# Columns of neighbouring weight tiles woven together in a two-layer decoder kernel

## What is computed

```python
qkv = (h @ w_qkv).reshape(B, S, 3, N_HEADS, HEAD_DIM)      # layer 0: 2048 x 6144
return out @ w_o                                           # both layers: 2048 x 2048
proj = h @ w_in                                            # layer 1: q, k, v, qi, ki, wi
u = h @ w_up                                               # both layers: 2048 x 11264
return (jax.nn.silu(gate) * val) @ w_down                  # both layers: 5632 x 2048
```

## Time and profile before

| | |
|---|---|
| median of 2 runs | 2218.64 us (2217.64 to 2219.65) |
| span of the profiled execution | 2216.0 us |
| outside the span, to the median | 2.6 us |
| TensorE busy with matmuls | 2209.4 us, 12470 matmuls |
| VectorE, ScalarE busy | 1484.4 us, 1177.3 us |
| weights loaded | 406.70 MB on SyncE's queue, 56.5% of the 16 DMA engines' time |
| granted TensorE clock | full in all of the span |

### The profile page before, as it was taken

The page is one execution under the profiler, slowest core; times in us unless marked ns, Lnnn a source line. Parts: engine busy times, 40 slices in busy tenths (PEclk is TensorE's granted clock), DMA queues, the critical chain, the costliest instruction groups (busy, mean ns, idle before and its releaser), DMA issues.

```text
span 2216.0 us, 34772 instructions
## 1 busy us (share of the span) xinstructions
PE 2209.4 (100%) x12470; PEld 1935.2 (87%) x12470; DVE 1484.4 (67%) x1753; ACT 1177.3 (53%) x1409; POOL 14.3 (1%) x21
## 2 busy tenths in 40 slices
PE   9999999999999999999999999999999999999999
PEld 8888898888888888888899888888888888888887
DVE  7666556677777777555578888667777777774443
ACT  7565555555555555444455466555555555553333
POOL 0000000000000000000010000000000000000000
PEclk9999999999999999999999999999999999999999
DMA  7555555555555555565566544555555656566664
GB/s 270 166 168 177 171 162 181 195 185 190 189 193 186 189 190 191 190 190 189 191 212 198 177 157 139 161 183 191 182 198 181 194 184 198 180 193 201 201 199 136
DMA packets 113829, 411.55 MB, mean 186 GB/s; under 512 B 12769, under 2 KB 13537, under 8 KB 113761
## 3 DMA queue, kind: packets, MB, share of 16 engines
q1 hardware_dynamic: 112320, 406.70, 56.5%
q10 hardware_dynamic: 1008, 2.30, 0.3%
q0 software_dynamic: 432, 1.57, 0.2%
HBM read 408.42 MB, written 2.10 MB: 185 GB/s over the span
## 4 chain that ended last, share of the span: by engine, by line
PE 99%; DMA 0%; SPq 0%; DVE 0%; ACT 0%; issue 0%; DVEq 0%
PE psum L1301 99%; DMA raw<-w_all 0%; PE psum L1621 0%; PE psum L1557 0%; DVE w_lo L747 0%; ACT w_hi L289 0%; SPq L237 0%; SPq L235 0%; DVE upad L822 0%; SPq L236 0%; SPq L234 0%; DVEq L83 0%
## 5 line engine op out<-in xcount | busy, mean ns | idle before, releaser
L747 DVE TENSOR_TENSOR w_lo<-raw,w_hi 128x1024 fp32r<-128x1024 f32 x769 | 935.6, 1224 | 678.6 <-ACT w_hi L289 672.8
L1301 PE MATMUL psum<-xg,w_hi 128*128 128x512 f32 (+1 forms) x3936 | 1358.3, 392 | 1.9 <-DVE w_lo L747 1.0
L289 ACT CAST w_hi<-raw 128x1024 fp32r<-128x1024 f32 x770 | 803.1, 1049 | 771.4 <-PE psum L1301 767.6
L1301 PE MATMUL psum<-xg,w_lo 128*128 128x256 f32 (+1 forms) x3920 | 1090.8, 278 | 0.0
L1301 PEld LDWEIGHTS psum<-xg,w_hi 128*128 128x128 f32 x3936 | 736.0, 187 | 156.7 <-issue 2.2
L1301 PEld LDWEIGHTS psum<-xg,w_lo 128*128 128x128 f32 x3920 | 742.6, 189 | 2.6 <-issue 2.2
L1301 PE MATMUL psum<-hid,w_hi 128*128 128x512 f32 x704 | 244.1, 391 | 0.0
L1301 PE MATMUL psum<-w_hi,hid 128*128 128x512 f32 x704 | 217.9, 390 | 0.0
L1301 PE MATMUL psum<-hid,w_lo 128*128 128x256 f32 x704 | 197.4, 280 | 0.0
L1301 PE MATMUL psum<-att,w_hi 128*128 128x512 f32 x512 | 178.8, 393 | 0.0
L1301 PEld LDWEIGHTS psum<-hid,w_hi 128*128 128x128 f32 x704 | 131.7, 187 | 28.6
(11 more groups left out here) (176 smaller groups left out, 1062.9 us busy)
## 6 DMA issues: line engine op xcount, KB each, us to landing
raw<-w_all SPq DMA_DIRECT2D x770, 512.0 KB, 3.8
xres<-x_in SPq DMA_DIRECT2D x3, 512.0 KB, 9.0
cst<-consts_in ACTq DMA_DIRECT2D x2, 768.0 KB, 6.6
raw<-w_all SPq DMA_DIRECT2D x2, 256.0 KB, 3.6
xres<-x_in SPq DMA_DIRECT2D x2, 256.0 KB, 3.8
out_t<-part POOLq DMA_DIRECT2D x1, 512.0 KB, 7.3
out_t<-conv POOLq DMA_DIRECT2D x1, 512.0 KB, 7.4
out_t<-gates POOLq DMA_DIRECT2D x1, 512.0 KB, 7.0
```

Of the source, the lines that this page charges most:

```text
L289: act.copy(w_hi[:, c % RING, :], raw[:, c % RING, :]).then_inc(hi_ready, 1)
L747: dve.tensor_tensor(w_lo[:, c % RING, :], raw[:, c % RING, :], f32(w_hi[:, c % RING, :]), ALU.subtract).then_inc(lo_ready, 1)
L1301: return pe.matmul(o, lhsT, rhs, start=start, stop=True, skip_group_check=True)
```

## The change

The host permutes the output features of the weights that `proj` and `proj_index` use as stationary operands (`_woven`): in each group of two tiles (four in the second output projection) column `j` of tile `a` goes to place `step * j + a`. On the chip the tile is then read with that step (`column_tile`), and what is multiplied with what is the same as before. Pieces, their order and their sizes stay, and so do the loads, the splits and all the instructions of ScalarE, VectorE, SyncE and GpSimd. TensorE's instructions stand in the same order with the same shapes, but for the line numbers; the step inside the access pattern of the stationary operand is all that differs.

Not woven are the KI projection (its pieces have a single tile for each row, step 1), the weighting of the indexer, and the weights that are moving operands (the values of both layers, the down projection of layer 1).

```diff
+            def column_tile(buf, s, row, ct, step):
+
+                if step == 1:
+                    return buf[:, s, row + ct * P:row + (ct + 1) * P]
+                if step == 4:
+                    return buf[:, s, row + ct:row + 4 * P:4]
+                pair = row + ct // 2 * 2 * P
+                return buf[:, s, pair + ct % 2:pair + 2 * P:2]
...
-                        w = slice(kk * cols + ct * P, kk * cols + (ct + 1) * P)
+                        hi, lo = (column_tile(buf, s, kk * cols, ct, step) for buf in (w_hi, w_lo))
...
-                        mm(psum[:, bank0 + ct, :], w_hi[:, s, w], act_in[:, k, :], first and kk == 0)
-                        last = mm(psum[:, bank0 + ct, 0:T], w_lo[:, s, w], act_in[:, k, 0:T])
+                        mm(psum[:, bank0 + ct, :], hi, act_in[:, k, :], first and kk == 0)
+                        last = mm(psum[:, bank0 + ct, 0:T], lo, act_in[:, k, 0:T])
...
-                        w = slice(kk * 256 + ct * P, kk * 256 + (ct + 1) * P)
+                        hi, lo = (column_tile(buf, s, kk * 256, ct, 2) for buf in (w_hi, w_lo))
...
-            out_groups(BASE_WO[1], 1, 8, att, 0, wo1_ready, l1_tail)
+            out_groups(BASE_WO[1], 1, 8, att, 0, wo1_ready, l1_tail, step=4)
...
+def _woven(w, step):
+
+    k, n = w.shape
+    w = w.reshape(k, n // (step * P), step, P)
+    return np.ascontiguousarray(w.transpose(0, 1, 3, 2)).reshape(k, n)
...
-               _pieces(v, 2, 512), _pieces(k, 4, 256), _pieces(q, 4, 256),
-               _pieces(a["wo1"][0], 2, 512)) + mlp(1))
+               _pieces(v, 2, 512), _pieces(_woven(k, 2), 4, 256), _pieces(_woven(q, 2), 4, 256),
+               _pieces(_woven(a["wo1"][0], 4), 2, 512)) + mlp(1))
```

More of the change, by code:

```diff
@@ L1301, in mm, with proj @@
                 return pe.matmul(o, lhsT, rhs, start=start, stop=True, skip_group_check=True)
-            def proj(c, i, per, bank0, act_in, kts, k0_, cols, first, by_tile=False, upper_free=None):
+            def column_tile(buf, s, row, ct, step):
[5 more added lines that the diff above has]
+                return buf[:, s, pair + ct % 2:pair + 2 * P:2]
+            def proj(c, i, per, bank0, act_in, kts, k0_, cols, first, by_tile=False, upper_free=None, step=2):
                 if by_tile:
@@ L1336, in proj_index @@
                             pe.wait_ge(xg_ready, 11)
-                        w = slice(kk * 256 + ct * P, kk * 256 + (ct + 1) * P)
+                        hi, lo = (column_tile(buf, s, kk * 256, ct, 2) for buf in (w_hi, w_lo))
                         both = xg[:, k0_ + kk, :].rearrange("p (a t) -> p a t", a=2)[:, :, TI:T]
-                        mm(out2, w_hi[:, s, w], both, first and kk == 0)
-                        last = mm(psum[:, bank0 + ct, 0:n], w_lo[:, s, w], xg[:, k0_ + kk, TI:T])
+                        mm(out2, hi, both, first and kk == 0)
+                        last = mm(psum[:, bank0 + ct, 0:n], lo, xg[:, k0_ + kk, TI:T])
                 last.then_inc(piece_used, 1)
@@ L1380, in settle, with out_groups @@
                     mm(psum[:, bank, 0:P], xg[:, 0, 0:P], xg[:, 1, 0:P], True)
-            def out_groups(base, layer, per, src, n0, ready, tail=None):
+            def out_groups(base, layer, per, src, n0, ready, tail=None, step=2):
                 for g in range(4):
@@ L1389, in out_groups @@
                         upper = ready(e) if g == 0 else None
-                        proj(base + g * per + e, None, 0, 4 * (g % 2), src, 2, 2 * e, 512, e == 0, upper_free=upper)
+                        proj(base + g * per + e, None, 0, 4 * (g % 2), src, 2, 2 * e, 512, e == 0, upper_free=upper, step=step)
                         if tail and g == 0:
@@ L1543, in mlp_layer @@
                     out_groups(base + UP, layer, FT // 2, hid, 4 + 2 * UPG,
-                               lambda e: hid_ready(layer, e))
+                               lambda e: hid_ready(layer, e), step=2)
                 else:
@@ L1666, in _ @@
             for e in range(2):
-                proj(L1_KI + e, None, 0, 2, xg, 8, 8 * e, P, e == 0)
+                proj(L1_KI + e, None, 0, 2, xg, 8, 8 * e, P, e == 0, step=1)
                 if e == 0:
@@ L1746 @@
     flat = lambda *p: [q.reshape(-1, P, PIECE) for q in p]
-    qkv = [_pieces(a["qkv"][0][:, n * D:(n + 1) * D], 4, 256) for n in range(3)]
+    qkv = [a["qkv"][0][:, n * D:(n + 1) * D] for n in range(3)]
+    qkv = [_pieces(qkv[n] if n == 2 else _woven(qkv[n], 2), 4, 256) for n in range(3)]
     two = _pieces(a["qkv"][0][:, 2 * D + 256:3 * D - 256], 2, 512)
@@ L1758, in mlp @@
         up = a["up"][layer]
-        both = np.concatenate([_pieces(up[:, :FF], 2, 512), _pieces(up[:, FF:], 2, 512)], axis=1)
-        return flat(both, _pieces(a["dn"][layer], 2, 512))
-    qip = _pieces(qi, 4, 256)
+        both = np.concatenate([_pieces(_woven(up[:, :FF], 2), 2, 512), _pieces(_woven(up[:, FF:], 2), 2, 512)], axis=1)
+        return flat(both, _pieces(a["dn"][layer] if layer else _woven(a["dn"][layer], 2), 2, 512))
+    qip = _pieces(_woven(qi, 2), 4, 256)
     w_all = np.concatenate(
-        flat(*l0, _pieces(a["wo0"][0], 2, 512)) + mlp(0)
+        flat(*l0, _pieces(_woven(a["wo0"][0], 2), 2, 512)) + mlp(0)
         + flat(qip[:1], _pieces(kk, 8, P), _pieces(np.pad(np.concatenate([wi, wi], axis=1), ((0, 0), (0, 2 * NH))), KT, 4 * NH), qip[1:],
-               _pieces(v, 2, 512), _pieces(k, 4, 256), _pieces(q, 4, 256),
-               _pieces(a["wo1"][0], 2, 512)) + mlp(1))
+               _pieces(v, 2, 512), _pieces(_woven(k, 2), 4, 256), _pieces(_woven(q, 2), 4, 256),
+               _pieces(_woven(a["wo1"][0], 4), 2, 512)) + mlp(1))
     assert w_all.shape == (NPIECES, P, PIECE)
```

## The result

The changed kernel takes 2278.6 us (median of 2 runs, 2278.58 to 2278.61) against 2218.6 before. The ratio is 1.0272, with a 95% interval from 1.0243 to 1.0302. It is 60 us slower. The forecast was no change, and 2278.6 lies above the range of 2120 to 2260.

What follows compares the result with a forecast made beforehand. TensorE's matmuls were taken as the only bound, with weight loads just covered. All parts cost 0: 2216.0 + 0 = 2216.0 us span, with 2.6 us outside 2218.6, forecast 2219 us; range 2120 to 2260.

Steps and rivals of the forecast that it cites:

- What bounds the kernel: Whole kernel: TensorE busy with matmuls 2209.4 of 2216.0 us at full clock; ScalarE and VectorE have time to spare.
- Host side, loads, splits, moving operand: cost 0: Transfers, cast, subtraction, moving operand, output and matmul count keep their form under permuted weights; cost 0.
- Loads with step 4: cost 0: Second output projection, 256 pairs: loads taken as costing the same as before, 0, between bounds of 0 and 26 us.
- Rival B: Second output projection: only step 4 slow, load 105 ns more, about 0.446 us a pair, 26 us, 2245 us; chance 0.18.
- Loads with step 2: cost 0: 4864 pairs (second output projection's 256 at step 4) and the indexer: load stays at 111 ns, cost 0.
- the fixed part of a matmul: Every fp32r matmul: some 13 ns beyond its columns, taken as unchanged by the size of the load.
- Rival E: Woven matmuls: the 13.4 ns over their columns shrinks as steps spread colliding reads; 81 us less, 2138 us; chance 0.26.
- Rival C: All stepped loads: 105 ns more per load, pairs from 0.346 to 0.446 us, 525 us more, 2744 us; chance 0.13.
- The range: Kernel time 2120 to 2260 us, leaving out the case of every step slow, under 2 in 10 outside.
- The indexer's pair: Indexer: a pair of 512 and 192 columns read as 0.281 us before, expected to stay so.
- What would show it: Timeline signs: unchanged 0.346 us a pair and 187 ns loads if right; another matmul distance in any woven stage if wrong.

Runs made afterwards that it cites:

- The wide runs: Both matmuls of a pair 512 columns wide: kernel before so widened outside the indexer 2736.5 us, changed kernel likewise 2803.8 us; also stage-by-stage probes, one at 2770.4 us.
- the narrow ones: Runs keeping pairs of 512 and 256 columns, with steps varied by stage or pairs disturbed; e.g. steps 1 and 2 alternating by stage, 2241.3 us.

## Why the prediction was wrong

- **What bounds the kernel** was right: TensorE's matmuls alone, at full clock, and the feeders never showed.
- **Host side, loads, splits, moving operand: cost 0** was right, by the unchanged stages and feeders.
- **Loads with step 4: cost 0** was the wrong end of its bounds. Rival B had the mechanism, the place and nearly the size: the load takes much longer, fits under the long matmul and not under the short one. It priced a pair at 0.446 us and the stage at 26 us; it is 0.470 us and 31 us. Where it is covered the load lasts 122 ns more (310 against 188), and not 105. That a load asks no more of SBUF than the moving operand does was my reason for 0, and that step failed. The load grows with the lines of four values that it touches, by 1.8 ns a line from step 2 to 4: with step 4 each value has a line to itself, which the moving operand, read in order, never asks for.
- **Loads with step 2: cost 0** failed too, by 6.7 ns a pair and 29 us before what the second output projection adds. The step that failed is the fixed part of a matmul. I took it as constant, because the loads of 32 columns left it alone, and let only a load longer than its cover show. The wide runs show that step 2 adds 6.7 ns to it with the load covered, and the narrow ones that it isn't a constant at all: it takes one of a few values for whole stages (346.7, 350.0 or 353.3 ns a pair), with step 1 as with step 2, and a single odd pair or piece can change it.
- **Rival E** looked for the effect at the right place, the fixed part, but with the wrong sign; whether two reads of TensorE collide there no run tells. **Rival C** is refuted: the load of step 2 grows by 5 to 9 ns, and the MLPs are at 0.353 and not at 0.446.
- **The range** took B and a small cost of step 2 as alternatives. They are in different stages and add up: 26 and 29 would have been 55 us. I had written that each ns on a step-2 load costs 4.9 us and did not put the sum of both into the range.
- **The indexer's pair** was read 4 ns low. A stretch of 8 us counts the matmuls that its ends cut, and by the distance of starts a pair had 284.6 ns and not 281. The forecast doesn't depend on it.
- **What would show it** named the stretches that did show it: another distance between matmuls in every woven stage and none in the down projection of layer 1.

What stays open: why step 2 adds 6.7 ns to a covered wide matmul, why the pairs lock into these rhythms, what decides between them on entry, and whether the kernel could have 346.7 ns a pair with step 2 in all stages. Shown is that single groups, and one half of layer 1's up projection, have it, and that the kernel's time moves with it.

## What to carry to other kernels

In this kernel a stationary float32 operand read with step 4 costs a load of 310 ns and not 188, and it shows where the matmul before it has only 256 columns to hide it. Step 2 lengthens the load by 5 to 9 ns and still wasn't free. Where TensorE is the bound and each matmul has a load of its own, compare the distance of starts stage by stage, in equal work, before a difference of 1% is put down to an edit: a change of order that does the same work moved this kernel by as much.

## What the runs showed of the hardware that I had not expected

- The kernel before, with one pair in the second piece of each group turned round, takes 2243.0 us for 2219.6: the same work, 1% apart, for the rhythm alone (353.3 against 346.7 ns a pair).
- A rhythm outlives the boundary of a piece, with its wait on a semaphore, for at least twenty pieces, and changes at a disturbance.
- With 512 columns in every matmul, loads of 64 columns make a pair slower than loads of 128 (460 against 453.3 ns), and so does a start two values off (460.9). With 512 and 256 columns the loads of 64 with step 1 are the fastest of all (340.6).
- A load with step 8 takes 19 ns more than one with step 4, though each value has a line of its own in both.
